# Moving the second layer's modulation out of the first stage of a two-layer backbone kernel

## What is computed

```
shift, scale, gate = jnp.split(jax.nn.silu(c) @ w_mod + b_mod, 3, axis=-1)
shift_c, scale_c, gate_c = jnp.split(jax.nn.silu(c_ctx) @ w_mod + b_mod, 3, axis=-1)
h_lat = rmsnorm(x, norm_g) * (1.0 + scale[:, None]) + shift[:, None]
h_ctx = rmsnorm(ctx, norm_g) * (1.0 + scale_c) + shift_c
s_lat = split_cols(h_lat @ w_in)
s_ctx = split_cols(h_ctx @ w_in)
...
x = x + gate[:, None] * y_lat
```

## Time and profile before

| | |
|---|---|
| median of 3 runs | 5987.77 us (5977.72 to 5989.83) |
| the profiled execution's own time | 5990.59 us |
| its span, first to last instruction | 5988.8 us |
| PE busy | 5438.1 us (91%) |
| DVE / ACT / POOL busy | 2914.2 / 1677.3 / 2310.4 us |
| mean granted TensorE clock | 0.940 of 2.4 GHz |
| modulation / projection0 / gates0, to the next stage's first instruction | 142.6 / 1163.4 / 46.3 us |

### The profile page before, as it was taken

How to read it: one execution, slowest core, us unless ns; L and a number is a source line. 1 busy time by engine, 2 the same in 40 slices (tenths; PEclk the granted TensorE clock), 3 DMA queues, 4 the chain that set the end, 5 groups by cost and what they waited for, 6 DMA issues and landing times. The chain is left out here.

```text
span 5988.8 us, 75051 instructions
## 1 busy us (share of the span) xinstructions
PE 5438.1 (91%) x26062; PEld 2873.6 (48%) x26096; DVE 2914.2 (49%) x4931; ACT 1677.3 (28%) x4031; POOL 2310.4 (39%) x1691
## 2 busy tenths in 40 slices
PE   3999999977988799998989999999578879999979
PEld 1444444536777433332435544444367754333334
DVE  0344454454777655551113455455557765555212
ACT  0111111111344244444002212212123332444411
POOL 0022122123444279998001112121234434999910
PEclk7999999986999899999999999999779987999989
DMA  8233323227222100000532333332452220000032
GB/s 303 71 102 100 102 96 104 95 96 220 86 96 96 64 1 8 8 6 12 238 114 93 105 100 102 102 100 96 138 182 96 91 72 18 1 8 8 4 126 84
DMA packets 386809, 530.67 MB, mean 89 GB/s; under 512 B 115106, under 2 KB 272602, under 8 KB 380102
## 3 DMA queue, kind: packets, MB, share of 16 engines
q1 hardware_dynamic: 360726, 453.14, 23.0%
q10 hardware_dynamic: 19728, 40.41, 1.8%
q0 software_dynamic: 6048, 33.11, 1.5%
HBM read 372.15 MB, written 154.08 MB: 88 GB/s over the span
## 5 line engine op out<-in xcount | busy, mean ns | idle before, releaser
L586 PE MATMUL psum<-group_W,projection_hT 128*128 128x512 f32 (+4 forms) x5016 | 1952.9, 546 | 5.9 <-DVE projection_hT L699 5.7
L586 PEld LDWEIGHTS psum<-group_W,projection_hT 128*128 128x128 f32 x5016 | 948.4, 190 | 973.7 <-issue 932.3
L2163 POOL TENSOR_TENSOR attention_PS<-attention_PS 128x1024 f32<-128x1024 f32 x548 | 1265.2, 2352 | 82.6 <-ACT attention_PS L2296 74.3
L2209 DVE TENSOR_REDUCE attention_mxp<-psum 128x1 f32<-128x512 f32 (+1 forms) x1016 | 654.4, 686 | 542.0 <-PE psum L2345 542.0
L441 POOL TENSOR_TENSOR projection_cx<-projection_cx,projection_cw 128x768 f32<-128x768 f32 x102 | 189.0, 1853 | 1685.0 <-DMA projection_cw<-in_ss_conv_w 1685.0
L2296 ACT ACTIVATE attention_PS<-psum 128x512 f32<-128x512 f32 (+1 forms) x1168 | 630.6, 591 | 718.1 <-PE psum L2399 687.6
L2345 PE MATMUL psum<-attention_QK 32*128 32x512 f32 (+1 forms) x2592 | 778.3, 629 | 8.6 <-DVE attention_mxp L2198 5.8
L2393 PE MATMUL psum<-attention_QK 32*128 32x512 f32 x2336 | 664.7, 643 | 0.0
L2411 PE MATMUL psum<-attention_PS,attention_va 128*64 128x512 f32 x2336 | 628.4, 617 | 0.0
L650 ACT ACTIVATE projection_ut<-psum 128x256 f32<-128x256 f32 (+2 forms) x322 | 127.5, 407 | 1421.2 <-PE psum L586 1412.0
L2529 PE MATMUL psum<-output_W,output_yT 128*128 128x512 f32 x1088 | 477.4, 597 | 21.3 <-DMA output_W<-in_w_out 21.3
(11 more groups left out here) (344 smaller groups left out, 6130.6 us busy)
## 6 DMA issues: line engine op xcount, KB each, us to landing
u<-projection_ut SPq DMA_DIRECT2D x240, 256.0 KB, 2.0
projection_cx<-xbc SPq DMA_DIRECT2D x306, 128.0 KB, 2.2
projection_cw<-in_ss_conv_w SPq DMA_DIRECT2D x102, 384.0 KB, 4.5
mixing_hg<-u SPq DMA_DIRECT2D x34, 1024.0 KB, 5.0
modulation_wm<-in_w_mod SPq DMA_DIRECT2D x12, 2048.0 KB, 8.6
group_W<-in_w_in SPq DMA_DIRECT2D x8, 2316.0 KB, 33.4
output_y<-y SPq DMA_DIRECT2D x34, 512.0 KB, 4.6
group_W<-in_w_in POOLq DMA_DIRECT2D x6, 2316.0 KB, 28.9
```

The costliest lines, as they stand in the source:

```text
L586: ins = nc.tensor.matmul(ps[n % RING][:, lo - c0:lo - c0 + w], hT[b][:, q], W[q][:, lo:lo + w], start=(q == 0), stop=(q == KT - 1))
L2163: G.tensor_tensor(SA[x % 2][:, rs, 0:w], one[:, rs, 0:w], PT[i % PTB][:, rs, 0:w], ALU.add) \
L2209: bk.release(V.tensor_reduce(mxp[x % 2][:, q:q + nn, 2 * pr + j, a], bk[job, j][:, 0:nn * (hi - lo)].rearrange("p (q n) -> p q n", q=nn), ...
```

## The change

It has four parts. First, modulation makes layer 0's modulation only (6 blocks); layer 1's is made in gates0 (`more`), with all six blocks of w_mod in tiles of their own, loaded by SP behind gates0's small loads. Second, the bias is no longer added by DVE: it is loaded as one row, `brow`, and a product of it with `orow` (two ones, else zeros) opens each bank (in modulation and in gates0). Third, in modulation SP issues w_in's row blocks between those of w_mod, and in projection PE runs the first tile's first five column blocks over the row blocks that came early before it waits for the others. Fourth, a stage takes its semaphores from one of two halves by turns, and clears its half with one instruction on POOL, without the second meeting of the engines.

```diff
     def clear(self, sems):
-        for s in sems:
-            self.nc.gpsimd.sem_clear(s)
-        self.nc.all_engine_barrier()
+        assert len(list(sems)) <= self.taken
+        lo = FIRST_SEM + HALF_SEMS * self.half
+        self.nc.gpsimd.sem_clear(range(lo, lo + self.taken))
+        self.half, self.taken = 1 - self.half, 0
...
 def modulation(k):
-    NB = 6 * DEPTH
+    NB = 6
...
-                for n in range(2, NB):
-                    block_in(n)
+                weights(range(0, 4))
+                block_in(2)
+                block_in(3)
+                weights(range(4, 5))
+                block_in(4)
+                block_in(5)
+                weights(range(5, KT))
                 sp.wait_ge(s["lb_l"], 1)
...
+                    T(ps[n % 2][0:32], orow[:], brow[:, n * 512:(n + 1) * 512], start=True, stop=False, skip_group_check=True)
...
 def projection(k, l):
-                pe.wait_ge(k.w_in, 16 * (KT + (KT - early) * l))
...
+                        if where == "context" and b == 0:
+                            for n in range(RING):
+                                pe.wait_ge(s[f"bank_free{n}"], 1)
+                                if l:
+                                    partial(b, n, kind, range(early))
+                            pe.wait_ge(k.w_in, 16 * (KT + (KT - early) * l))
+                            for n in range(RING):
+                                partial(b, n, kind, range(early if l else 0, KT))
...
 def gates(k, l):
+                if more:
+                    sp.dma_start(brow[:], k.x["b_mod"][l + 1].unsqueeze(0)).then_inc(s["bias_in"], 16)
+                    wl = k.x["w_mod"][l + 1].rearrange("(k p) n -> p k n", p=P)
+                    for n in more:
+                        sp.dma_start(wm[n][:], wl[:, :, n * 512:(n + 1) * 512]).then_inc(s[f"wm_in{n}"], 16)
+                    sp.dma_start(pair[:], k.x["c_pair"]).then_inc(s["bias_in"], 16)
                 sp.wait_ge(s["out_ready"], 1)
...
+                if more:
+                    pe.wait_ge(s["bias_in"], 32)
+                    pe.wait_ge(s["ones_made"], 2)
+                modulated(more[0:2])
                 pe.wait_ge(s["m_done"], 1)
```

More of the change, by code:

```diff
@@ L593, in _ @@
                         pe.wait_ge(s["hT_ready"], r * 2 + (b + 1))
-                        for n in range(5):
+                        if where == "context" and b == 0:
[6 more added lines that the diff above has]
+                                partial(b, n, kind, range(early if l else 0, KT))
+                        for n in () if where == "context" and b == 0 else range(RING):
                             products(r, b, n, kind)
@@ L865, in gates @@
         pick = k.sb(c, "pick", [P, 2, P])
+        more = range(6) if l + 1 < DEPTH else ()
+        GATE = 4
+        wm = [k.sb(c, f"wm{n}", [P, KT, 512]) for n in more]
+        part = [k.sb(c, f"part{n}", [P, 512]) for n in more]
+        brow = k.sb(c, "brow", [1, 3 * D])
+        orow = k.sb(c, "orow", [1, 32])
+        grow = k.sb(c, "grow", [2, D])
+        pair = k.sb(c, "pair", [P, 2])
         ps = k.bank
@@ L872, in gates @@
         HALF = NT // 2
+        PIECES = (0, 4, 5)
         side = lambda d: slice(32 * d, 32 * d + H)
@@ L994, in _, with parts @@
                         .then_inc(s["row_copied"], 1)
+                def parts(some):
+                    for n in some:
+                        act.wait_ge(s["mod_mm"], n + 1)
+                        A(part[n][:], ps[1 + n % 2][:], ACT.Copy).then_inc(s["part_copied"], 1)
+                parts(more[0:2])
                 for a in range(2):
@@ L1005, in _ @@
                 ins.then_inc(s["end_copied"], 1)
+                parts(more[2:4])
                 act.wait_ge(s["sum_mm"], 2)
@@ L1045, in _, with modulated, collected @@
                     ins.then_inc(s["sum_mm"], 1)
+                def modulated(some):
+                    for n in some:
+                        pe.wait_ge(s[f"wm_in{n}"], 16)
+                        pe.wait_ge(s["row_copied"], len(jobs))
+                        if n >= 2:
+                            pe.wait_ge(s["part_copied"], n - 1)
+                        T(ps[1 + n % 2][0:32], orow[:], brow[:, n * 512:(n + 1) * 512], start=True, stop=False,
+                          skip_group_check=True)
+                        for q in range(KT):
+                            j = q % 4
+                            ins = T(ps[1 + n % 2][32 * j:32 * j + 32], k.sc[:, q], wm[n][:, q], start=(0 < q < 4), stop=(q >= 4),
+                                    skip_group_check=True)
+                        ins.then_inc(s["mod_mm"], 1)
+                def collected(some):
+                    for n in some:
+                        pe.wait_ge(s["part_copied"], n + 1)
+                        for m in range(4):
+                            ins = T(ps[3][:, 8 * n + 2 * m:8 * n + 2 * m + 2], part[n][:, m * P:(m + 1) * P], pair[:],
+                                    start=True, stop=True)
+                        ins.then_inc(s["col_mm"], 1)
+                if more:
+                    pe.wait_ge(s["bias_in"], 32)
+                    pe.wait_ge(s["ones_made"], 2)
+                modulated(more[0:2])
                 pe.wait_ge(s["m_done"], 1)
```

115 lines of the change are left out of this document (74 added, 41 removed).

## The result

The changed kernel takes 5933.2 us (median of 4 runs, 5928.92 to 5936.52) against 5985.4 us for the kernel before (4 runs, 5977.72 to 5989.83). The ratio is 0.9916, with a 95% interval from 0.9904 to 0.9929. A second set of five runs of it, in another job, gave 5932.78 us and 0.9914. The forecast was 5931, in a range from 5906 to 5952. The profiled execution took 5931.59 us, with a span of 5929.7 us and a mean granted clock of 0.948.

The account below looks back on a forecast made before the run. PE bounds the stages' long middles, which the change leaves alone; gains lie between them. A -38, B -51, C -9 and D +41 sum to -57: 5933.6 us for the profiled execution, 5931 as median, range 5906 to 5952.

Parts of the forecast that it names:

- A: Between stages: second meeting and single semaphore clears go, one clear on POOL stays; -38 us at 13 places.
- Rival 2: Between stages: instruction fetches that the clears had covered come into sight, A gives back 20 us, 5951 us; chance 0.09.
- B: First stage: new load order on SP keeps transfers flowing, end at 89.4 us instead of 140.7; -51 us.
- Rival 3: First stage and gates0: memory gives 360 GB/s, not 408 to 434; B loses 12 us, D 4; 5947 us; chance 0.04.
- The term of the element stores: First stage: four small stores of single elements cut the flow to 111 GB/s for 6 us; 4.5 us lost.
- C: projection1: transposes and products start on the early row blocks without waiting for late ones; -9 us, bounds -7 and -11.
- D: gates0: layer 1's modulation moves here and PE waits for `pair` behind six blocks; +41 us, from +32 to +52.
- Rival 1: gates0: `pair` is not held back behind the blocks, D loses its first 18.9 us; 5912 us; chance 0.09.
- rivals 4 and 5: gates0: blocks load far slower; at 120 GB/s 6005 us (slower), at about 150 GB/s 5984 (no change); chance 0.02 each.
- the 18.9 us for `pair`: gates0: M's transposes start 18.9 us late, at 1351.5, behind PE's wait for `pair` and two modulation blocks.
- the 6.9 us for `cs`: gates0: two more blocks and ACT's copies stand ahead of `cs`, which DVE needs; adds 6.9 us.

Follow-up runs that it names:

- the copies late: Changed kernel with ACT's copies of the second pair of modulation blocks in gates0 moved behind the exponent, `pair` still last in SP's queue: 5923.71 us.

## Why the prediction was right, step by step

**A** was right in size and in cause: 38.4 us were read from one row, 39.0 went, and undoing it brought 38 back. Rival 2, code that comes into sight, did not happen: POOL's first instruction of each stage starts 0.2 to 0.4 us after the clear begins. Its premise was also misread. The prediction says that it found hardly another fetch beside that of the earlier trace rows; in the kernel before, packets of instructions fall into six of the 13 stretches of clears and meeting. Whether the meetings hid them is not shown; without the meetings no wait of this kind is to be seen, and the whole of A was gained.

**B** was right to 1.3 us in the profile, in size and in the wait that ends last. PE started at 19.97 where 19.4 was forecast, and w_in's last packets ended near 83 where the terms give 83.7. Rival 3 is refuted by the flow, 411 to 435 GB/s here and 389 in gates0, where it put 360. The term of the element stores was mis-sized: 4.5 us for them and 1.2 for the gate rows' store make 5.7, and from 83 to the end of SP's wait near 91 it was 8. I had priced them by the flow that they displace; at the end of a queue they have a quiet tail instead, with packets over by 84.5 us. What the stage's end waits for in it is shown only so far as that it isn't the count of elements. Another place in the queue would not have saved it: the four stores cost 6.0 us of flow in the middle as well.

**C** had the mechanism right and was mis-sized: -5.6 instead of -9, just outside its bounds. The first transposes came 8.04 us after the stage's start, as the forecast's 3137.1 says, and the products at 12.9, as forecast. The tile was forecast to be ready near 3164, 34.9 us after the start; PE took it up at 35.6, since the products ahead of it took 20.45 us instead of 19.3, at a granted clock of 0.81 in their first 15.9 us. That is 0.7 of the 3.4 us that were missing. The step that failed is another: the forecast let PE stand for that tile at no price beyond the wait. PE stood 2.27 us, and behind it the granted clock fell to the 1.2 GHz level and was 0.69 on the mean from 3137.5 to 3143: transposes of 1.75 us instead of 1.07, and 12 products 3.82 us instead of 2.76, 1.7 us together. In the kernel before they stood in this row:

```profile
3173.63 2.76 PE L586 MATMUL psum<-group_W,projection_hT 128*128 128x256 f32 x12
```

The last 1 us lies in the rest of the stage and in rounding, and I cannot place it.

**D** was right to 1.2 us, with errors that cancel. Six blocks flowed at 389 GB/s, not 408, so `pair` was in at +39.0 instead of +37. The four blocks on the path ahead of the pieces took 7.8 and 7.3 us instead of 8.5 each; the last two took 10.8 instead of 8.5, all at 1.2 GHz; the end values 1.4 us less and the tail 1.4 less than forecast. `cs` made DVE wait 5.51 us where 6.9 was forecast. The forecast's 1343.0 for `pair` stands 1 us above its own 1311.2 + 30.8, without a word on it; without that 1 us the error would be 3 us. Rival 1, that `pair` slips by, is refuted by the 22.34 us, and rivals 4 and 5 with it. And these 39.8 us are of a profile in which gates0 was short: in the second it was 3.1 us longer.

The prediction counted the 18.9 us for `pair` and the 6.9 us for `cs` as separate terms, 25.8 in sum. By the medians that was sound: taken away one at a time they give 19.5 and 9.5 us, together 28.7. By gates0 in one profile each they give 12.9, 5.4 and 27.9, with the clock's draw in them.

The four parts were forecast at -57 and made -54.5 in the profiles, and the medians differ by 52.2. The forecast started from a median of 5987.77 us for the kernel before; beside the changed kernel it measured 5985.4, 2.4 us less. So 4.8 us less were gained than forecast, from a start 2.4 us lower, and 5931 is missed by only 2.2. That it is so near is in part luck; that it lies in the range is not.

## What to carry to other kernels

Order a DMA queue by when each tile is first needed, not by size: a 1 KB constant behind 12.58 MB of weights cost 19 us of the kernel's time. When such a wait goes, look for the next one: with `pair` first, DVE's wait for `cs` grew from 5.51 to 8.89 us, and the order on ACT was worth 9 us more. Judge an edit of a few us by the medians and by the piece of the timeline that it touches, not by the length of a stage in one profile: gates0 moved by 3 us with no edit at all. Clears of single semaphores and an additional meeting at each stage's end are pure idle time, 3 us a stage here, and were cheaper to win than anything inside the stages.

## What the runs showed of the hardware

- Stores of single 4-byte elements are awkward wherever they stand. At the end of the queue the stage waited some 6 us after the last packet; in its middle they cost 6.0 us of flow; on another queue they held the flow at 168 GB/s for 16 us. Twice as many at the end cost at most 1.5 us more. The landing of the large load ahead of them was late too, 28.0 us after its issue. What the chip does in the quiet tail stays open.
- One clear of a range of semaphores took 0.14 to 0.35 us on POOL; the single clears, with the meeting, took 3.0 us a stage.
- SP could issue the six 2 MB loads of gates0 only in 21.25 us, and `pair` behind them took 5.29 us to issue, where a load ahead of them took 0.29 to 0.43: the issuing engine can stand for the loads before. I take it that the queue was full; no run shows it.
- The same 16 products took 1.92 or 3.64 us in gates0 by the granted clock. A wait stood ahead of the fall in projection1 (2.27 us), but in gates0 with the copies late the clock was 0.50 for 10.00 us in which PE was busy throughout. So a wait of PE is not the only thing after which the lower level is found, and no run here separates what else it hangs on.
